# Value products of the short attentions: one 128-query product per key block in place of two 64-query column pieces

## What is computed

```python
# window attention (layer 0), A_WINDOW = 128, chunks of 64
s = einsum(q, k) * HEAD_DIM ** -0.5 - slope * dist          # float32
p = softmax(concatenate([s, sink]))[..., :-1]
o = einsum('bchgqk,bckhd->bcqhgd', p, v)                    # value products
# memory attention (layers 0 and 1), MEM_LEN = 256
s = einsum('bshd,bmhd->bhsm', q, mk) * HEAD_DIM ** -0.5
o = einsum('bhsm,bmhd->bshd', softmax(s), mv)               # value products
```

## Time and profile before

| | us |
|---|---|
| median of 3 runs | 3659.0 |
| lowest, highest | 3647.3, 3659.1 |
| span of the profiled execution | 3662.1 |
| TensorE busy in it | 3333.1 (91%) |
| short attentions of layer 0, first to last product | about 790 to 974 of the span |
| short attention of layer 1 | about 2653 to 2712 of the span |

### The profile page before, as it was taken

One profiled execution on the slowest core, in us unless ns is written; L12 is line 12 of the kernel. 1 busy time (PEld: TensorE's weight loads), 2 busy tenths in 40 slices (PEclk: granted clock), 3 DMA queues, 4 the chain that ended last, 5 costly groups with the idle time before them and its releaser, 6 DMA issues. The chain is left out here.

```text
span 3662.1 us, 90162 instructions
## 1 busy us (share of the span) xinstructions
PE 3333.1 (91%) x36876; PEld 2902.3 (79%) x36876; DVE 2130.1 (58%) x5023; ACT 1898.0 (52%) x3756; POOL 815.7 (22%) x900
## 2 busy tenths in 40 slices
PE   5899999989888888997797999997789999999899
PEld 5777899978777776885665898897678888888787
DVE  7100100028788893331199998996967777777322
ACT  5122211126677773221287766755468888888311
POOL 3222200001377770001101532521510000000000
PEclk9999999989899999998899999998899999999999
DMA  5333421159412314345421436335563333331432
GB/s 195 109 115 118 144 65 65 48 112 238 131 46 75 83 39 146 114 154 195 116 58 46 138 113 182 135 96 163 207 183 88 91 84 84 92 86 51 153 112 85
DMA packets 368257, 416.91 MB, mean 114 GB/s; under 512 B 51816, under 2 KB 272616, under 8 KB 366952
## 3 DMA queue, kind: packets, MB, share of 16 engines
q1 hardware_dynamic: 303096, 318.55, 30.1%
q10 hardware_dynamic: 64768, 92.81, 7.0%
HBM read 247.21 MB, written 164.10 MB: 112 GB/s over the span
## 5 line engine op out<-in xcount | busy, mean ns | idle before, releaser
L1402 PE MATMUL s_o<-s_v,s_pT 128*64 128x65 f32 (+1 forms) x13056 | 436.6, 224 | 9.6 <-issue 9.4
L1402 PEld LDWEIGHTS s_o<-s_v,s_pT 128*64 128x64 f32 x13056 | 402.0, 138 | 46.0 <-issue 24.6
L230 PE MATMUL s_acc<-s_wh,s_hT 128*128 128x256 f32 (+1 forms) x1408 | 430.6, 306 | 7.8 <-ACT s_parts L653 4.6
L232 PE MATMUL s_acc<-s_wh,s_hT 128*128 128x256 f32 (+1 forms) x1408 | 429.8, 305 | 0.0
L231 PE MATMUL s_acc<-s_wl,s_hT 128*128 128x256 f32 (+1 forms) x1408 | 429.7, 305 | 0.0
L230 PE MATMUL s_acc<-s_hT,s_wh 128*128 128x512 f32 x880 | 349.8, 397 | 57.3 <-DVE s_wl L329 25.8
L1565 ACT ACTIVATE s_probs<-s_probs,s_nmx 128x512 f32<-128x512 f32 (+3 forms) x640 | 388.8, 662 | 12.0 <-DVE s_nmx L1630 12.0
L1614 DVE CUSTOM_DVE_ANT_0 s_probs<-s_s,s_scores 128x512 f32<-128x512 f32 (+3 forms) x640 | 364.4, 607 | 8.9 <-issue 5.1
L2375 DVE TENSOR_SCALAR_CACHE_REDUCE s_scratch<-s_scores,s_thr 128x384 uint8<-128x384 f32 (+4 forms) x320 | 365.3, 1209 | 1.1
L231 PE MATMUL s_acc<-s_hT,s_wh 128*128 128x512 f32 x880 | 347.7, 395 | 0.0
L232 PE MATMUL s_acc<-s_hT,s_wl 128*128 128x512 f32 x880 | 347.5, 395 | 0.0
(11 more groups left out here) (278 smaller groups left out, 7180.2 us busy)
## 6 DMA issues: line engine op xcount, KB each, us to landing
fm<-s_parts ACTq DMA_DIRECT2D x120, 512.0 KB, 2.8
s_y<-y SPq DMA_DIRECT2D x32, 640.0 KB, 5.9
y<-s_g SPq DMA_DIRECT2D x18, 1024.0 KB, 5.8
kc<-s_parts SPq DMA_DIRECT2D x32, 512.0 KB, 3.3
s_w<-in_o_fm SPq DMA_DIRECT2D x25, 512.0 KB, 4.5
s_w<-in_o_w_in SPq DMA_DIRECT2D x12, 1024.0 KB, 5.6
s_qh<-fm SPq DMA_DIRECT2D x42, 256.0 KB, 3.2
s_ql<-fm SPq DMA_DIRECT2D x42, 256.0 KB, 3.7
```

The costliest lines, as they stand in the source:

```text
L230: nc.tensor.matmul(out, sh, mh, start=(j == 0), stop=False)
L232: ins = nc.tensor.matmul(out, sl, mh, start=False, stop=(j == n - 1))
L1402: last = nc.tensor.matmul(o_ps[half * HD:(half + 1) * HD, 0:w], pT[half][:, x0:x0 + HD], v[:, g.u.kbs[g.a + x], vc:vc + w], start=(g.first ...
```

## The change

The loop over `r` is gone. One product per head and key block takes all 128 queries as its stationary operand and writes 128 partitions. The numbers that are multiplied and summed are the same.

```diff
                         for k in range(m):
                             v0 = (kb + k) * HD if d.window else k * W + h * HD
-                            for r in range(0, P, HD):
-                                at = x * W + k * P + r
-                                last = nc.tensor.matmul(o_ps[n % 2][r:r + HD, h * HD:(h + 1) * HD],
-                                                        pT[p % R][:, at:at + HD], v[t][:, v0:v0 + HD],
-                                                        start=(k == 0), stop=(k == m - 1), skip_group_check=True)
+                            at = x * W + k * P
+                            last = nc.tensor.matmul(o_ps[n % 2][:, h * HD:(h + 1) * HD], pT[p % R][:, at:at + P],
+                                                    v[t][:, v0:v0 + HD], start=(k == 0), stop=(k == m - 1),
+                                                    skip_group_check=True)
                     last.then_inc(fed, 1)
```

## The result

| | before | after |
|---|---|---|
| median of 11 runs each, us | 3651.4 | 3665.6 |
| lowest, highest | 3647.3, 3659.1 | 3662.5, 3670.0 |
| span of the profiled execution | 3662.1 | 3668.2 |

The ratio after to before is 1.0031, 95% interval 1.0023 to 1.0040: some 11 us slower, 8 to 15 by the interval. The two medians of the table differ by 14.2 us. The forecast was 3668 with a difference of +9 us, and the two agree.

The account below looks back on a forecast made before the run. TensorE was taken to bound the two short-attention calls. Ordinary pairs +8.3 us, one-key-block pairs -0.6 and low-clock pairs +1.5 gave about +9 us, so 3668 us against the median 3659.0; range 3648 to 3684.

Parts of the forecast that it names:

- What bounds the calls: Both short-attention calls: TensorE alone is full, so its loss per pair, or gain up to 0.49 us per unit, reaches the call.
- the rival in which the transfers or another engine set when the calls end: Short-attention calls: something else sets the time, so no difference or a few us, 3659 to 3668; chance 0.08 (shared).
- What is removed: Value products per pair: 16 records of 64 columns, 0.88 us, of which about 0.3 is switching to column halves and back.
- the case that the border costs stay: Ends of each value series: the borders keep their 0.3 us, a pair loses 0.37 us, kernel near 3705.
- What is added: Value products per pair: eight records of 128 stationary columns, each stepping 0.11 us by its load, for two in 0.058.
- the first rival: Value products: undivided ones load like transposes, step 0.06 us, a pair gains 0.28, kernel 3627; chance 0.12.
- the second rival: Value products: load and product stop overlapping, step 0.16 us, a pair loses 0.52, kernel 3723; chance 0.08.
- The sum per pair: Last score product to first transpose: 0.12 + 0.77 + 0.06 = 0.95 us against 0.88, 0.07 more per pair.
- The sum for the kernel: All 128 pairs of both calls: 8.3 - 0.6 + 1.5, about +9 us; by the bounds of the step +8 to +18.
- Pairs with one key block: Four of the 128 pairs: section 0.65 us before, 0.51 after, a gain of 0.14 each, 0.6 together.
- the low clock: Some five pairs at the calls' starts, at 1.2 GHz: 0.4 us more each, partly hidden behind first transfers, +1.5 us.
- The absolute time: Whole kernel: +9 us on the median 3659.0 of the kernel before gives 3668 us.

Follow-up runs that it names:

- grouped pieces: The kernel before, with the value products of both pairs of a unit issued together in one series: 3639.6 us, ratio 0.9952.

## Why the prediction was right, step by step

**What bounds the calls.** Right. TensorE's loss per pair arrived in full at the next stages' first products, and the waits of VectorE and ScalarE only grew. That rules out the rival in which the transfers or another engine set when the calls end. The gain with grouped pieces confirms the other direction: VectorE's wait of 0.49 us could be used up to 0.30 without a new bound.

**What is removed.** Right. The 16 records are 8 steps of 0.058 (32 records in 16 steps, 8 in 4), and the switch there and back, put at about 0.3 us, measured 0.29 and 0.34. Both borders lost it. By the starts of loads, the way in shrank from 0.33 to 0.12 us; the way out, from the last value load to the second transpose load, from 0.26 to 0.18. Of the rivals, the case that the border costs stay is out.

**What is added.** Right in mechanism, a little small in size. Loads of 192 ns mean, where 190 was named for this case and 140 for the first rival; a step that does not change when half the columns are streamed, which rules out the second rival. The step is 0.1115 us over many records, and 0.110 was used. The Trainium skill ("TensorE: Matmul & The Clock Gate", section "LDWEIGHTS (loading the stationary operand)") would make it 107 ns; the trace has 4% more. One reading behind the first rival was weak from the start: the transposes' loads of 140 ns start 0.109 us apart within a series of four, so the duration of a load does not give its step, and loading like a transpose would not by itself have given 0.06.

**The sum per pair.** The step of the prediction that was mis-sized is this sum: 0.07 us more per pair, where the periods show 0.09 in the window sets and 0.08 in the memory sets. Its seven steps were put at 0.77; by the loads the first is 0.12 and the other six are 0.112, 0.79 in all. With 0.12 ahead and 0.06 behind them that is 0.97 us against 0.95 predicted, while the 0.88 before stood. The period of 1.98 came as 1.99 to 2.00.

**The sum for the kernel.** At 0.084 us, the mean over 98 pairs of the steady stretches, 123 pairs at the high clock lose 10.3 us, where the prediction has 119 x 0.07 = 8.3. Pairs with one key block: the predicted section is 0.51 us, and so it is (806.69 to 807.20):

```profile
806.69 0.28 PE L2053 MATMUL s_s<-s_kl,s_q 128*128 128x256 f32 x1
806.81 0.55 PE L2084 MATMUL s_o<-s_v,s_pT 128*128 128x64 f32 x4
807.20 0.61 PE L2066 MATMUL s_t<-s_ident,s_probs 128*128 128x128 f32 x4
```

At the low clock the pair that answers to the earlier trace rows:

```profile
2661.90 0.41 PE L2053 MATMUL s_s<-s_kl,s_q 128*128 128x256 f32 x1
2662.11 1.58 PE L2084 MATMUL s_o<-s_v,s_pT 128*128 128x64 f32 x8
2663.53 0.61 PE L2066 MATMUL s_t<-s_ident,s_probs 128*128 128x128 f32 x4
```

The section is 1.42 us from product to transpose against 1.04. Because the first product now starts 0.21 and not 0.34 us behind the last score product, the net loss is 0.25, not 0.4. And there are not five such pairs but one: in both kernels only the first series of each call falls into the low clock, and in the first call that pair has one key block and loses nothing (0.97 us from the last score product to the transpose before, 0.95 after). In the kernel before, the granted clock is 1.00 from 806.2 us of the span on in the first call and from 2662.9 on in the second; the second pair starts its value products at 806.76 and 2664.08. So this term was +1.5 in the prediction and is about +0.3. Together 10.3 - 0.6 + 0.3 = 10.0 us, and the steady parts of the calls show 9.8 to 10.3. That the sum of +9 came so close owes something to luck: 2 us too few for the steps, which is the term that was mis-sized, and 1 us too many for the low clock partly cancel. What the stages behind the second call add, if anything, it had at nothing.

**The absolute time.** 3668 rests on a median of before of 3659.0, which came out at 3651.4 with more runs, 7.6 us lower. The medians then differ by 14.2 us where +9 was said, 5.2 more. The two nearly cancel, and 3668 against 3665.6 is in this respect luck. The periods and the two calls, and not the absolute time, show how good the working was.

**What was said to show it.** 1008 records with 128*128, as said. The section in stamps 0.96 for 0.90 predicted. The next stage at 988.7 for 988. VectorE's wait went to 0.79, not 0.6. The unit's period grew by 0.16 to 0.17; the rest is a second wait that was overlooked. The copy behind the scaling, in the kernel before and then in the changed one:

```profile
883.31 0.69 DVE L2106 COPY s_pT<-s_t 128x512 f32<-128x512 f32 x1
```

```profile
886.16 0.69 DVE L2105 COPY s_pT<-s_t 128x512 f32<-128x512 f32 x1
```

Before, the scaling ended at 882.78 + 0.42 and the copy started 0.11 us later, when the transposes were there; after, it starts as soon as the scaling is done (885.77 + 0.42 = 886.19, stamped at 886.16). The long series puts VectorE's whole slack in front of the scaling: 0.49 + 0.11 = 0.60 before, 0.79 after.

## What to carry to other kernels

A plain float32 product with 128 stationary columns costs its load, 0.11 us a record, with 64 streamed columns as with 32; cut into two column halves of 64 that alternate, the same work takes 0.058. To enter and leave the halves costs 0.3 us, so by estimate (0.3 / 0.053) pieces pay from about six undivided records in a row on. The runs bracket it: with 4 in a row the undivided form is 0.14 us faster, with 8 the pieces are 0.08 to 0.09 faster, with 16 they are 0.50 faster (a unit of 3.53 against 4.03). More is won by longer series of pieces, not by giving them up, as long as the engine that waits for them has slack. When two shapes of an operation are compared, price the series and its borders apart: here they are 0.4 us in favour of one side and 0.3 us in favour of the other, and only the small difference is seen in the time.

## What the runs showed of the hardware that was not expected

- **The clock can stay low for a whole stage while TensorE never rests.** The changed kernel's second call runs at a granted clock of 1.00 from about 2663 us on. With 32 in place of 64 streamed columns in its value products (and VectorE's reading changed to fit) it ran at 0.50 (1.2 GHz) to its end, with TensorE and its loads at 10.00 of 10 us, and lasted 115 to 116 us against 70, in ten of fourteen runs by their times. In the first call the same narrow records ran at the high clock (the mean from 870 us on is 1.00 with them), in the window sets and in the memory set. The engine's busy time does not show this; the clock column does.
- **Work of one column half runs ahead past work of the other.** With all pieces of one half first, three of eight of the second half still ran beside the first half's: 0.74 us from first start to last, 13 steps of 0.058 and not 16.
- **The switch has a price on both sides.** There and back was 0.29 to 0.34 us between three arrangements of the same products. The larger part lies on the way in, where the first piece's load starts 0.33 us behind the last score load in place of 0.12. This agrees with the Trainium skill ("TensorEngine Tiling (Array Packing)", section "Key Properties"), where a change of mode drains the engine but has no price.
